# Twelve modulation blocks moved to layer 0's attention, and eight weight units placed 48 columns further on

## What is computed

```python
for l in range(DEPTH):                                # the first block, DEPTH = 2
    shift_x, scale_x, gate_x = ada_modulation(c, w_mod[l], b_mod[l])
    hx = modulate(rmsnorm(x, norm_w[l]), shift_x[:, None], scale_x[:, None])
    px = split_proj(hx @ w_in[l])
...
    merged = sum(jax.nn.sigmoid(g) * (br @ w_branch[i])
                 for i, (g, br) in enumerate(zip(gates, (r, s, f, a))))
    return merged @ w_out
...
for i in range(DEPTH):                                # the second block
    mod = (c_act @ ada_w[i] + ada_b[i])[:, None, :]   # 6 * 1024 values from a 1024 x 6144 matrix
    sh_m, sc_m, gt_m, sh_f, sc_f, gt_f = jnp.split(mod, 6, axis=-1)
    h = rmsnorm_2(x, norm_g[i, 0]) * (1.0 + sc_m) + sh_m
```

## Time and profile before

| | us |
|---|---|
| runs | 1732.79, 1733.70, 1739.43 |
| median | 1733.7 |
| the profiled execution | 1734.11 |
| its span, first to last instruction | 1732.3 |

### The profile page before, as it was taken

One profiled execution on the slowest core, in us unless ns is written; L12 is line 12 of the kernel. 1 busy time (PEld: TensorE's weight loads), 2 busy tenths in 40 slices (PEclk: granted clock), 3 DMA queues, 4 the chain that ended last, 5 costly groups with the idle time before them and its releaser, 6 DMA issues.

```text
span 1732.3 us, 28134 instructions
## 1 busy us (share of the span) xinstructions
PE 1689.6 (98%) x10612; PEld 1475.4 (85%) x10612; DVE 1392.7 (80%) x2532; ACT 883.6 (51%) x1530; POOL 0.2 (0%) x4
## 2 busy tenths in 40 slices
PE   7999999999999999999999999999999999999998
PEld 4788887777888888898888999999899888889997
DVE  7799996546789998889787689877898767779874
ACT  5322324456333233453346755568766657566663
POOL 0000000000000000000000000000000000000000
PEclk9999999999999999999999999999999999999999
DMA  9683211211667776645333289744555544346553
GB/s 342 216 310 100 92 55 49 97 38 37 234 235 258 246 264 229 232 149 168 102 119 98 82 280 321 267 134 153 191 198 195 183 158 153 117 146 209 195 192 111
DMA packets 224774, 301.32 MB, mean 174 GB/s; under 512 B 6000, under 2 KB 188656, under 8 KB 224256
## 3 DMA queue, kind: packets, MB, share of 16 engines
q1 hardware_dynamic: 224640, 299.52, 51.6%
HBM read 298.45 MB, written 1.05 MB: 173 GB/s over the span
## 4 chain that ended last, share of the span: by engine, by line
PE 88%; DVE 6%; ACT 3%; issue 2%; DMA 1%; DVEq 0%; ACTq 0%
PE bank L706 21%; PE bank L711 21%; PE bank L708 21%; PE bank L1092 4%; PE bank L1094 3%; PE bank L1093 3%; PE bank L682 2%; PE bank L683 2%; PE bank L684 2%; DVE w_lo L2190 2%; PE bank L937 1%; PE bank L948 1%; PE bank L960 1%; PE bank L1159 1%; PE bank L1222 1%
## 5 line engine op out<-in xcount | busy, mean ns | idle before, releaser
L2190 DVE TENSOR_TENSOR w_lo<-ring,w_hi 128x1024 fp32r<-128x1024 f32 (+1 forms) x432 | 489.8, 1141 | 174.7 <-ACT w_hi L1408 172.5
L1408 ACT ACTIVATE w_hi<-ring 128x1024 fp32r<-128x1024 f32 (+1 forms) x432 | 425.6, 991 | 182.9 <-PE bank L711 90.4
L706 PE MATMUL bank<-h_hi,w_hi 128*128 128x256 f32 (+2 forms) x2086 | 372.9, 321 | 1.4 <-ACT w_hi L1408 1.4
L711 PE MATMUL bank<-h_hi,w_lo 128*128 128x256 f32 (+2 forms) x2086 | 366.9, 318 | 0.3
L708 PE MATMUL bank<-h_lo,w_hi 128*128 128x256 f32 (+2 forms) x2086 | 366.6, 318 | 0.0
L706 PEld LDWEIGHTS bank<-h_hi,w_hi 128*128 128x128 f32 x2086 | 305.1, 188 | 34.9 <-issue 2.7
L711 PEld LDWEIGHTS bank<-h_hi,w_lo 128*128 128x128 f32 x2086 | 305.8, 188 | 30.4 <-DVE w_lo L2190 0.7
L708 PEld LDWEIGHTS bank<-h_lo,w_hi 128*128 128x128 f32 x2086 | 305.8, 188 | 29.8
L1395 ACT ACTIVATE work<-bank 128x512 f32<-128x512 f32 (+1 forms) x134 | 67.2, 520 | 244.2 <-PE bank L711 164.2
L1395 ACT ACTIVATE arena<-bank 128x256 f32<-128x256 f32 (+4 forms) x119 | 55.2, 468 | 199.1 <-PE bank L711 122.0
L2492 DVE SCALAR_TENSOR_TENSOR arena<-arena,params 128x512 f32<-128x512 f32 (+1 forms) x240 | 130.5, 614 | 0.0
(11 more groups left out here) (320 smaller groups left out, 2116.5 us busy)
## 6 DMA issues: line engine op xcount, KB each, us to landing
ring<-in_w_in SPq DMA_DIRECT2D x86, 1024.0 KB, 5.5
arena<-in_ada_w_t SPq DMA_DIRECT2D x96, 512.0 KB, 5.9
ring<-in_ffn_w_up SPq DMA_DIRECT2D x44, 1024.0 KB, 5.0
ring<-in_ffn_w_down SPq DMA_DIRECT2D x20, 1024.0 KB, 5.1
ring<-in_w_branch SPq DMA_DIRECT2D x32, 512.0 KB, 4.7
arena<-in_w_mod_t SPq DMA_DIRECT2D x32, 512.0 KB, 4.9
ring<-in_gla_w_in SPq DMA_DIRECT2D x12, 1024.0 KB, 5.2
ring<-in_w_out SPq DMA_DIRECT2D x8, 1024.0 KB, 6.4
```

Of the source, the lines that this page charges most:

```text
L706: pe.matmul(out[:, 0:n], w[0][:, k, :], hi(k, n), start=k == 0, stop=False)
L711: m = pe.matmul(out[:, 0:n], w[1][:, k, :], hi(k, n), start=False, stop=k == tiles - 1)
L1408: nc.scalar.activation(hi, src, ACT.Copy)\
L2190: step(nc.vector.tensor_tensor(lo, src, hi.bitcast(F32), ALU.subtract), f"lo {u}", *(["used " + stream[w_units[u][0]][0]] if w_units[u][3] ...
```

## The change

1. **Twelve blocks of `ada` move.** Six new slabs of 1 MB, two blocks each, are put into the weight stream behind the six slabs of `sc_z`, `ret_z` and `att_z` of layer 0 (`mod_slab`). Each block is done by DVE right behind the low part of one unit, beginning with `sc_z 0.1` (`mods_behind`), from the ring buffer itself. `mod_plan[1, pair]` has one block instead of two for the pairs 4 to 15.
2. **Some units are put aside.** `w_hi` and `w_lo` grow by 64 columns, `h_hi` and `h_lo` shrink by 64. A unit in the set `aside` that falls on part 3 stands 48 columns further on (`w_of`). Its difference to the tokens is then 0 instead of 48. The rules pick eight units: `cf_g 1.1`, `gate 1.sc.3`, `gate 1.sc.7`, `out 1.3`, `ffv 0.3`, `ffv 0.13`, `ffg 1.3` and `ffg 1.13`. The rule for the gates of the last two branches picks none, as their units fall on parts 0 and 1.
3. **The recurrent layer's input** (`g_hi`, `g_lo`, 16 units of 258 columns) is packed in steps of 258 columns from column 48 on: its difference is now 48, 50, ... 62.

```diff
-        h_flat = [sbuf(n, KT * (2 * S + SPARE), F32R)[:] for n in ("h_hi", "h_lo")]
+        h_flat = [sbuf(n, KT * (2 * S + SPARE) - ASIDE, F32R)[:] for n in ("h_hi", "h_lo")]
...
-        g_hi, g_lo = tiles_at(0, LATE_N, S + SPARE)
+        g_hi, g_lo = tiles_at(BESIDE, LATE_N, LATE_N)
...
+        last_part = (PARTS - 1) * KT * P
+        aside_hi, aside_lo = (w[:, last_part + BESIDE:last_part + BESIDE + KT * P].rearrange("p (t n) -> p t n", t=KT)
+                              for w in w_flat)
...
+        def w_of(u):
+
+            return (aside_hi, aside_lo) if u in aside else (w_hi[u % PARTS], w_lo[u % PARTS])
...
+        att_blocks = [take_blocks(adas, 2) for _ in range(ATT_MODS)]
...
         for pair in range(1, pairs):
-            mod_plan[1, pair] = take_blocks(adas, 2 if pair >= KT // 2 else 0)
+            mod_plan[1, pair] = take_blocks(adas, 1 if pair >= KT // 2 else 0)
...
+        def mod_slab(slab, tile):
+
+            (_, l, c), last = att_blocks[slab]
+            src = io["ada_w_t"][l][P * c:P * c + 2 * P, :].rearrange("(j p) k -> p j k", p=P)
+            stream.append((f"w mods {slab}", src, (2, D)))
+            u = unit_of[tile]
+            mods_behind[u], mods_behind[u + 1] = (slab, 0), (slab, 1)
...
                     section(l, n, i, run)
+                    if l == 0 and n == "sc_z":
+                        mod_slab(i, f"sc_z 0.{2 * i + 1}")
...
+                    if l == 0:
+                        mod_slab(2 + 2 * j + i, f"{a} 0.{2 * i + 1}")
...
+        aside = {*aside_units([f"{a} 1.{i}" for a in ("cf_g", "cf_a") for i in range(1, BT)], 1),
+                 *aside_units([f"gate 1.{b}.{i}" for b in MERGE_ORDER[:2] for i in range(KT)], 2),
+                 *aside_units([f"gate 1.{b}.{i}" for b in MERGE_ORDER[2:] for i in range(KT)], 1),
+                 *aside_units([f"out 1.{i}" for i in range(1, KT)], 1)}
+        for l in range(2):
+            aside |= {*aside_units([f"{a} {l}.{i}" for i in range(2, 12) for a in ("ffg", "ffv")], 1),
+                      *aside_units([f"{a} {l}.{i}" for i in range(12, 22) for a in ("ffg", "ffv")], 1)}
...
                     fed["n"] += 1
+                    if u in mods_behind:
+                        slab, j = mods_behind[u]
+                        n = slab_of[f"w mods {slab}"]
+                        dve.wait_ge(*landed(n))
+                        modulate_block(*att_blocks[slab][j], slot_of(n)[:, j, :], stats)
+                        if j:
+                            vector.now[f"used w mods {slab}"] = vector.n
```

More of the change, by code:

```diff
@@ L58 @@
 SPARE = 16
+ASIDE = 64
 LATE_IN = 8
@@ L80 @@
 MOD_SLOTS = 4
+ATT_MODS = 6
 MOD_LATER = 2
@@ L167, in program @@
         h_hi, h_lo = tiles_at(BESIDE, 2 * S, 2 * S)
-        g_hi, g_lo = tiles_at(0, LATE_N, S + SPARE)
+        g_hi, g_lo = tiles_at(BESIDE, LATE_N, LATE_N)
         x_hi, x_lo = tiles_at(BESIDE, S, S)
-        y_hi, y_lo = tiles_at(KT * (S + SPARE), S, S)
+        y_hi, y_lo = tiles_at(KT * (S + SPARE) - ASIDE, S, S)
         in_hi, in_lo = (both_hi, h_hi, x_hi), (both_lo, h_lo, x_lo)
-        w_parts = [sbuf(n, PARTS * KT * P, F32R)[:].rearrange("p (u t n) -> p u t n", u=PARTS, t=KT) for n in ("w_hi", "w_lo")]
+        w_flat = [sbuf(n, PARTS * KT * P + ASIDE, F32R)[:] for n in ("w_hi", "w_lo")]
+        w_parts = [w[:, 0:PARTS * KT * P].rearrange("p (u t n) -> p u t n", u=PARTS, t=KT) for w in w_flat]
         w_hi, w_lo = ([w[:, i] for i in range(PARTS)] for w in w_parts)
+        last_part = (PARTS - 1) * KT * P
+        aside_hi, aside_lo = (w[:, last_part + BESIDE:last_part + BESIDE + KT * P].rearrange("p (t n) -> p t n", t=KT)
+                              for w in w_flat)
         r_hi, r_lo = ([w[:, i].rearrange("p t n -> p (t n)").rearrange("p (k n) -> p k n", k=ROW_K) for i in range(PARTS)]
@@ L468, in unit_parts @@
             src = slot_of(n)[:, :, P * half:P * half + P]
-            return src, w_hi[u % PARTS][:, 0:src.shape[1], :], w_lo[u % PARTS][:, 0:src.shape[1], :]
+            hi, lo = w_of(u)
+            return src, hi[:, 0:src.shape[1], :], lo[:, 0:src.shape[1], :]
         def section(l, name, i, run):
@@ L514, in mod_in @@
             return mod_landed[n % MOD_SLOTS], 16 * (n // MOD_SLOTS + 1)
+        mods_behind = {}
+        def mod_slab(slab, tile):
[4 more added lines that the diff above has]
+            mods_behind[u], mods_behind[u + 1] = (slab, 0), (slab, 1)
         for l in range(2):
@@ L535, in gate_slab @@
                            IN_COL["gates"] + D * BRANCHES[b] + 256 * i, run)
-            for a in ("ret_z", "att_z"):
+            for j, a in enumerate(("ret_z", "att_z")):
                 for i in range(2):
                     section(l, a, i, run)
+                    if l == 0:
+                        mod_slab(2 + 2 * j + i, f"{a} 0.{2 * i + 1}")
             for i in range(2 if l else 0):
@@ L588, in program, with aside_units @@
         ffn_slabs(1)
+        def aside_units(names, n):
+            return [unit_of[name] for name in names if unit_of[name] % PARTS == PARTS - 1][:n]
+        aside = {*aside_units([f"{a} 1.{i}" for a in ("cf_g", "cf_a") for i in range(1, BT)], 1),
[5 more added lines that the diff above has]
+                      *aside_units([f"{a} {l}.{i}" for i in range(12, 22) for a in ("ffg", "ffv")], 1)}
         def first_tiles(l):
@@ L671, in unit @@
                 pe.wait_ge(*vector.did(f"lo {u}"))
-                return w_hi[u % PARTS], w_lo[u % PARTS], f"used unit {u}"
+                return *w_of(u), f"used unit {u}"
             def part(h, s0):
@@ L702, in project @@
                     pe.wait_ge(*scalar.did(f"hi {u}"))
-                    w = w_hi[u % PARTS], w_lo[u % PARTS], f"used unit {u}"
+                    w = *w_of(u), f"used unit {u}"
                     out = open_bank(name)
```

## The result

| us | before | the changed kernel |
|---|---|---|
| median | 1735.37 (17 runs) | 1742.83 (17 runs) |
| least | 1732.53 | 1737.86 |
| the profiled execution, its time | 1734.11 | 1742.83 |
| its span | 1732.3 | 1741.0 |

The ratio is 1.0035, with a 95% interval of 1.0025 to 1.0044: the change costs some 6 us. By the bound of the prediction (0.5%) that is still no change, but the time lies above the range of 1725.0 to 1734.5 and has the other sign than forecast. Two of the 17 runs of the changed kernel, 2109 and 4365 us, and one of the 17 before, 4365 us, stand apart from all others and are not in the ratio; without them the medians would be 1742.42 and 1734.76. The other 15 runs of the changed kernel fall into two groups, six from 1737.9 to 1740.5 us and nine from 1741.9 to 1744.1.

A forecast was written before the change was run, and what follows sets the result against it. The kernel was taken to be bound by PE's matmuls (busy 98%). Terms -1.6 - 2.8 + 0 - 0.9 + 0.6 + 0 = -4.7 us gave 1729.0 us, range 1725.0 to 1734.5 us.

The forecast's parts named there:

- the term of the addresses: Units put aside, behind `cf_g 1.1` and `out 1.3`: they lead slow matmul streams back to the quick pace, -0.9 us.
- The unit's own cost: Eight units put aside: their matmuls at difference 0 take up to 6 ns longer each, +0.6 us, between 0 and 1.2.
- The aside units lead into the slow pace: Rival, chance 0.08: streams behind units put aside turn slow, 24 x 4.1 ns per unit of 256 columns; 1744 us.
- The wait at the end of the merge: End of layer 1's merge: moving twelve blocks away shortens PE's wait of 2.8 us, -1.6 us.
- The clock behind it: Matmuls behind the wait ending layer 1's merge: the clock no longer falls to 1.2 GHz, -2.8 us.
- The clock falls all the same: Rival, chance 0.20: the clock is still low behind the wait ending layer 1's merge; 1731.8 us.
- Layer 0: Layer 0, 256 to 380 us: the twelve blocks moved there are covered by DVE's waits for PE, 0 us.
- Layer 0 pays: Rival, chance 0.05: DVE waits for a slab or late scores make PE wait in layer 0; 5 us, 1734 us.
- The 258 columns: Recurrent layer's input, 384 matmuls: the new layout's differences change nothing, 0 us, with 2.2 us possible either way.

## Why the prediction was wrong

**The step that failed** is the term of the addresses. It said of the units put aside that "their likely work is to lead the stream back to the quick pace", and took -0.9 us for it. Units at difference 0 do the reverse: behind `ffv 0.3` and `ffg 1.3` they lead a quick stream into the slow pace, +4.0 and +4.3 us. In streams that were slow already they changed nothing: `cf_g 1.1` and `out 1.3`, from which I had expected 1.0 and 0.4 us, gave 0. The 1.0 us would not have come even from a quick stretch: in the five profiles that have one behind `cf_g 1.1`, PE loses it again in the wait for ACT at 792 us. I had counted half of it, for fear of a missing low part; it was the whole, and it was ACT. Two errors lie in the term. From the quick 227 ns of the 512-column matmuls at difference 0 I took that this difference is a quick one, but at 256 columns it is the slowest of the four tried: 120 ns, against 113.3 or 117.7 at 48, 118 at 32 and, at 16, the pace that the stream has. And I read what the code might be after as evidence of what it does, in a place where no row had the case. The row next to it, of 258 columns that run through difference 0 at 119 to 120 ns, pointed the right way; I used it for the unit's own cost only.

**The unit's own cost**, +0.6 us (0 to 1.2), was right in size. It is 24 x (120.0 - 113.3) = 0.16 us in a quick stream and 24 x (120.0 - 117.7) = 0.06 us in a slow one. Three of the eight stand in quick ones in the profile (`gate 1.sc.7`, `ffv 0.3`, `ffg 1.3`): 0.8 us in all.

**The rival "The aside units lead into the slow pace"** was the right one, at a chance of 0.08. Its 1744 us had the mechanism, the place and the price of a unit (24 x 4.1 ns; measured 24 x 4.4). It wrongly counted the stretch behind `cf_g 1.1`, which was slow before. It gave one up-projection 4.3 us, which is close to what each of them lost (4.0 and 4.3). That its sum came within 2 us of the measured time is in part luck: it charged about 150 units with 15 us where the units brought 8.3, and it had no slow merge (+3.4 us), which comes without such units too. The evidence that it held against itself, "most stretches at 48 are quick", says nothing about what a jump to 0 does to them, and "no stretch at difference 0 keeps a slow pace" was of 512 columns.

**The wait at the end of the merge**: -1.6 us was forecast, between 1.2 and 2.8, and the first matmul behind it moved by 1.84 us against the last one ahead of it. With the blocks alone it is 1.19 + 0.54 = 1.73 us. **The clock behind it**: -2.8 us, measured -2.64, and -(3.57 - 0.54) = -3.0 us with the blocks alone; the window shows 1.00. Together -4.5 us, or -4.8, for the -4.4 forecast, in single profiles; by the ratio of the runs the blocks alone give -2.9 us (-4.7 to -1.0). So "The clock falls all the same" was wrong. What the changed kernel's own profile alone would not have told is that a slow merge shortens this wait too: the units alone have -1.78 and -2.64 us there, with no block moved. In the changed kernel's profile the -4.5 can't be put down to the blocks; that they do it in a quick merge is shown by the blocks alone.

**Layer 0**: 0 us, measured 0.08 us from 62.73 to 760.53, with PE busy for 123.82 us in 256 to 380 us as before. "Layer 0 pays" was wrong. **The 258 columns**: 0, and nothing measured that could be told from it.

**The sum.** Of the profiled executions: +1.0 at the start, +0.3 up to the merge's second pair, +3.4 in the slow merge, -4.5 at its end, +4.0 and +4.3 in the up-projections and +0.2 between and behind them, 8.7 us, the difference of the two spans. With a quick merge it would be some 3.4 us less. The two groups of runs of the changed kernel are about that far apart (their middles are 1739.4 and 1743.2), though only a run of the upper one has a profile, so that the merge is what parts them is not shown.

**What stays open.** The merge is slow in four of the twelve profiles, in kernels with and without units put aside, from one of two short stops at its beginning on; nine of 15 runs of the change lie in the upper group, while nine of the 11 runs without the units lie under 1730.7 us. Whether the two gate units put aside make a slow merge likelier was not tried alone. Nor do the traces show why a difference of 0 slows: that the reads of tokens and weights meet in one place of the memory is an argument, not a reading. And every experiment moved weights while the tokens of these units stood at 48, so that it is the difference and not the weights' own place modulo 64 columns was not tested at 256 columns.

**A version that beats both**: the moved blocks without units put aside, 0.998 of before [0.9971, 0.9989]. With the eight units 16, 32 or 64 columns further on it is the same within the intervals.

## What to carry to other kernels

When a kernel is all matmuls, count them in unbroken stretches: a pace per matmul, at a clock of 1.00, is a number of its own beside waits and the clock, and 4% of it in two stretches was the loss here. Ask of a change in addresses what it does to the stream behind the place, not only in it, and price it by a row of the same size of matmul. And take a change of two parts as two experiments: one part here was worth -3 us and the other cost more than 9. And before a quicker stretch is counted as a gain, look at what PE waits for behind it: behind `cf_g 1.1` the whole gain went into the next wait.

## What was not expected of the hardware

- The same stream of 256-column matmuls, with a weight load for each, has two paces at the same clock and the same addresses: 113.3 ns and 117.7 ns. Each is kept for up to 100 us and more. A stall of under 1 us can be followed by either (the rows at 1007 us). Inside an unbroken stream the pace changed only at units put aside, in all twelve traces.
- At 256 columns and a difference of 0 a matmul takes 120 ns, and a unit of them leaves the stream at 117.7. At 16 and 32 units have left it at 113.3. At 512 columns it is the other way round: 227 ns at 0 and 234 at 48.
- The Trainium skill, "TensorE: Matmul & The Clock Gate", section "Part 2: What happens when you issue a matmul", holds that loading the next weights takes nothing from the running matmul's reads of SBUF. The runs disagree so far as this: with equal instructions in equal order on PE, the address of the weights of eight units alone made 1730 us or 1743.
- The granted clock stayed at 1.00 behind waits of 0.98 to 1.09 us at the end of the merge, and was 0.51 behind 2.82 us. A wait of 1.92 us can go either way. Before, it left the clock up; in the kernel with the units shifted by 64 columns the same wait, as long, was followed by a low clock, and so was one of 1.90 us with 27 units at difference 32. In the ten other profiles the wait at this place, 1.71 to 1.92 us, left it up. The timeline row and the window of the units shifted by 64 columns:

```profile
998.51 0.73 PE L744 MATMUL bank<-arena_r,w_hi 128*128 128x256 f32 x4 [1.92 <-ACT w_hi L1446]
```

```profile
998.00:1004.00 6.00, 5.49 (x34) 5.49 (x35) 5.51 (x14) 3.87 (x6) 0.00 (x0) 0.72 0.27 87
```

So rows 9, which the prediction took as evidence for a clock that stays, was weaker evidence than it looked; the waits behind which the clock stayed up in every profile looked at were about half as long.
